# Order of the expert blocks in the mixture-of-experts stage: four pairs first, then one overflow block and one pair in turn

## What is computed

```python
g_val, g_idx = lax.top_k(g_prob, 1)                 # best of 4 groups
e_val, e_idx = lax.top_k(in_group, MOE_TOPK)        # two of its 4 experts
...
hid = jax.nn.silu(jnp.einsum('td,edf->tef', t, w1)) * jnp.einsum('td,edf->tef', t, w3)
out = jnp.einsum('tef,efd->td', hid * combine[..., None].astype(hid.dtype), w2)
```

## Time and profile before

| | |
|---|---|
| median of three runs | 1314.01 us |
| the profiled execution's own time | 1310.76 us |
| its span in the profile | 1308.9 us |
| mean granted TensorE clock | 0.97 |
| TensorE matmuls busy | 1189.5 us, 91% of the span |
| VectorE, ScalarE, GpSimd busy | 49%, 29%, 14% |
| DMA engines, share of the SP queue q1 | 49.9% |
| expert stage of layer 0, from up(0) to the end of down(12) | 603.8 to 758.8 us |
| the same of layer 1 | 1122.8 to 1279.1 us |

### The profile page before, as it was taken

The page is one execution under the profiler, slowest core; times in us unless marked ns, Lnnn a source line. Parts: engine busy times, 40 slices in busy tenths (PEclk is TensorE's granted clock), DMA queues, the critical chain, the costliest instruction groups (busy, mean ns, idle before and its releaser), DMA issues.

```text
span 1308.9 us, 15046 instructions
## 1 busy us (share of the span) xinstructions
PE 1189.5 (91%) x4903; PEld 638.3 (49%) x4903; DVE 645.2 (49%) x1372; ACT 376.2 (29%) x954; POOL 186.1 (14%) x281
## 2 busy tenths in 40 slices
PE   5999999999999999978999939999889897899990
PEld 3566665656666554444344424433554444344440
DVE  2367668667676643463233251068755425322223
ACT  2144444444443320021122122112264532121110
POOL 1012232323232330001000030011200000100002
PEclk9999999999999999998999969999989999999996
DMA  9941992643724625785999866000380015799976
GB/s 327 326 128 49 350 304 72 241 157 108 248 97 167 258 80 205 297 330 190 412 421 421 354 211 233 1 0 1 83 303 1 1 72 218 281 416 420 420 309 227
DMA packets 102714, 285.94 MB, mean 218 GB/s; under 512 B 18224, under 2 KB 51296, under 8 KB 86384
## 3 DMA queue, kind: packets, MB, share of 16 engines
q1 hardware_dynamic: 82816, 245.65, 49.9%
q10 hardware_dynamic: 13776, 22.57, 5.2%
q0 software_dynamic: 6048, 16.79, 3.6%
HBM read 270.24 MB, written 27.85 MB: 228 GB/s over the span
## 4 chain that ended last, share of the span: by engine, by line
PE 74%; DVE 8%; DMA 6%; ACT 3%; DVEq 3%; issue 2%; SPq 2%; POOL 1%; ACTq 1%; POOLq 0%
PE bank L738 60%; DMA wts<-in_moe_w 2%; PE bank L909 2%; PE bank L1200 2%; DVE work L1707 1%; DMA work<-in_ada_w 1%; ACT xn L1658 1%; PE bank L1087 1%; DMA work<-slot_rows,work 1%; DVE wts L1707 1%; PE bank L1251 1%; PE bank L1049 1%; DVE xn L2255 1%; SPq L453 1%; PE bank L1264 1%
## 5 line engine op out<-in xcount | busy, mean ns | idle before, releaser
L738 PE MATMUL bank<-wts 128*128 128x512 f32 (+1 forms) x1312 | 458.8, 501 | 0.5 <-DVE work L1707 0.5
L738 PE MATMUL bank<-wts,work 128*128 128x512 f32 (+1 forms) x1088 | 376.1, 595 | 14.8 <-DVEq L2096 6.8
L738 PEld LDWEIGHTS bank<-wts 128*128 128x128 f32 x1312 | 243.7, 190 | 178.5 <-issue 163.4
L738 PEld LDWEIGHTS bank<-wts,work 128*128 128x128 f32 (+1 forms) x1088 | 148.8, 166 | 216.1 <-issue 200.6
L1707 DVE SCALAR_TENSOR_TENSOR work<-work,bank 128x256 f32<-128x256 f32 x58 | 24.3, 419 | 183.8 <-ACT work L1552 162.8
L1334 ACT ACTIVATE work<-bank 128x512 f32<-128x512 f32 (+2 forms) x120 | 62.8, 538 | 167.0 <-PE bank L738 125.4
L738 PE MATMUL bank<-work 128*64 128x512 f32 (+2 forms) x336 | 104.8, 576 | 6.6 <-DVE work L2065 4.9
L1707 DVE SCALAR_TENSOR_TENSOR work<-work 128x512 f32<-128x512 f32 (+4 forms) x121 | 93.8, 776 | 27.9 <-ACT work L1621 20.5
L1707 DVE SCALAR_TENSOR_TENSOR wts<-wts,cond 128x1024 f32<-128x1024 f32 x68 | 87.8, 1292 | 4.1
L1552 ACT ACTIVATE work<-bank 128x256 f32<-128x256 f32 x26 | 10.0, 384 | 226.7 <-PE bank L738 226.7
L696 POOL DMA_INDIRECT work<-xn_rows,work x26 | 26.1, 1005 | 261.6 <-PE bank L1087 217.0
(11 more groups left out here) (233 smaller groups left out, 1291.5 us busy)
## 6 DMA issues: line engine op xcount, KB each, us to landing
wts<-in_moe_w SPq DMA_DIRECT2D x90, 1024.0 KB, 23.1
wts<-in_ada_w SPq DMA_DIRECT2D x10, 4096.0 KB, 13.3
work<-in_moe_w SPq DMA_DIRECT2D x24, 1024.0 KB, 24.5
wts<-in_ssd_w_in SPq DMA_DIRECT2D x15, 1024.0 KB, 11.3
slot_rows<-work ACTq DMA_DIRECT2D x26, 512.0 KB, 7.8
xn<-in_moe_w SPq DMA_DIRECT2D x12, 1024.0 KB, 16.1
wts<-in_ssd_w_in SPq DMA_DIRECT2D x16, 512.0 KB, 12.4
work<-running_sums ACTq DMA_DIRECT2D x32, 256.0 KB, 3.6
```

Source lines behind the costliest of these rows:

```text
L738: return pe.matmul(out, lhsT, rhs, start=(k == 0), stop=(k == n - 1))
```

## The change

The tuple `BLOCK_AT` alone is altered. Everything that is derived from it follows: the slots, the order of loads, of gathers and of products.

```diff
-BLOCK_AT = (0, 1, 2, NP, 3, NP + 1, 4, NP + 2, 5, NP + 3, 6, NP + 4, 7) + tuple(range(NP + SURE, NB))
+BLOCK_AT = (0, 1, 2, 3, NP, 4, NP + 1, 5, NP + 2, 6, NP + 3, 7, NP + 4) + tuple(range(NP + SURE, NB))
```

## The result

The changed kernel took 1317.09 us (median of 8, 1316.6 to 1318.39) against 1314.43 of the kernel before (8 runs, 1312.59 to 1315.96), a ratio of 1.0022 with a 95% interval of 1.0012 to 1.0032. A second set of runs gave 1.0035 (1.0022 to 1.0048). Of 1314 us these ratios are 2.9 and 4.6 us. So the change makes the kernel slower, by 3 to 5 us, where I had said 9.6. The direction and the place were right, the size was too large by a factor of 3.3 against the one and 2.1 against the other.

What follows compares the result with a forecast made beforehand. Late in both expert stages TensorE and the DMA engines were taken as full at once, so the loads' lead counts. Terms 3.0 + 3.5 + 3.1 = 9.6 us on 1310.76 give 1320.4, or 1323.5 as median; range 1317 to 1328.

Steps and rivals of the forecast that it cites:

- The mechanism: End of both expert stages: up(11) comes to need load 39 instead of 36 and waits, by 3.0 and 4.8 us; up(12) does not wait.
- "Place 12" in layer 0: Expert stage of layer 0: up(12) begins at 745.0 instead of 741.96, +3.0 us, passed to the end in full.
- I keep the landing times of before by number: Weight loads of both layers: each load number lands when it did before, since only its number in the queue sets its landing.
- no load is issued later than the one of its number before: Weight loads of both layers: the same slots or more are free at each place; no size given.
- rival (d): DMA queue: deeper reserve fills holes, so neither place 11 nor 12 waits; -1.4 us at most, 1312.6; chance 0.03.
- Rival (c): Place 11: load 39 lands as its row says, at 731.5 and 1251.7; together +2.5 us, 1316.5; chance 0.10.
- low reading of a w1's landing: Load 39 before, a w1: reads only 0.8 and 0.7 us behind load 38; early parts of load 40 may fill its count.
- Place 12 in layer 1: Expert stage of layer 1: up(12) begins at 1265.8 instead of 1262.32, +3.5 us, the old wait of 1.32 us gone.
- The clock term: TensorE behind the gap at up(11): clock drops in layer 1, +3.1 us; 0 in layer 0, with 3.1 kept for the range.
- The sum: Whole kernel: 3.0 + 3.5 + 3.1 = 9.6 us slower, 1323.5 us; chance of this forecast 0.40.

## Why the prediction was right and where it was wrong

**The mechanism** was as predicted: the end of the order moves the last load that place 11 needs from number 36 to 39, up(11) waits for it in both layers, and up(12) no longer waits. No other place waits for a load in either profile, place 9 included, for which I had allowed up to 0.5 us. The run with the end alone exchanged and the run with places 3 to 10 alone show that only the end costs anything. The runs with lighter loads show that nothing but the supply carries the cost, the low clock behind the wait included.

**The term "Place 12" in layer 0**, +3.0 us, is the largest error in proportion. The stage became 1.3 us longer. The landing of load 39 was set too late by 1.3 us (129.4 against 128.1 after up(0)), and up(11) was ready 0.3 later than in the earlier trace rows (730.76 - 603.97 = 126.8 against 730.28 - 603.79 = 126.5), so the gap was 1.4 and not 3.0. When a wait is the difference of two nearly equal times, an error of 1% in one of them halves it.

**The step that failed** first is the sentence that I keep the landing times of before by number, with what it rests on, that only the number of a load in the queue sets its landing. Number sets the landing closely, as the run with the end alone shows (both waits within 0.05 us). It did so there because the front part was that of before. With the new front part load 39 landed 1.3 us earlier than I had taken in layer 0 and 0.6 in layer 1, and load 40 1.6 and 0.6 us earlier than in the mean of the four profiles of before. The lead is there early: load 14 lands at 50.6 and 53.0 us, against 51.9 to 54.3 and 53.4 to 54.1 before. I had read from the earlier trace rows that the DMA engines are busy throughout, but these rows show the late part alone. Windows over the first 20 us from up(0) of layer 0, before and changed:

```profile
603.79:623.79 20.00, 18.34 (x92) 7.95 (x94) 5.25 (x18) 4.17 (x11) 1.98 (x3) 1.00 0.60 234
```

```profile
603.97:623.97 20.00, 18.34 (x92) 7.93 (x94) 5.26 (x18) 4.17 (x11) 1.99 (x3) 1.00 0.64 251
```

The engines are busy for 0.60 of this time, so here the queue is not long, and the new order fills part of the hole: 17 GB/s more over 20 us are 0.34 MB, which at 420 GB/s is 0.8 us (an estimate from these rows). All four profiles of before have 232 to 234 GB/s there, both of the changed kernel 251. In layer 1 it is 313 to 325 against 337 and 338. Two things move into the hole. The first load is issued 7.1 us after up(0) instead of 7.8, since no expert number has to be read for it, and load 2 lands 0.7 us earlier. And the gather for place 3 moves the rows of a pair, 476 KB in layer 0, where it moved 68 KB before. The first alone is not enough. With all pairs first, load 1 is issued at 7.1 as well, but load 14 lands at 53.8 and 55.2 us. There the gathers of places 3, 4 and 5 are all those of pairs, where the changed kernel has two of them. So the gathers on the way count too, and not the number of the load alone. How the gain divides between the two is not shown. Nor is it true that no load is issued later than the one of its number before: loads 5 and 13 are issued 0.7 us later. They landed no later for it.

This is what rival (d) had in mind, loads that come earlier because the DMA had holes. It had the direction right, and of the 3 and 4.8 us that it needed 1.3 and 0.6 came. The prediction had also priced loads that are 1 us faster, with 1 us less in layer 0 and little in layer 1, and for layer 0 that is roughly what happened.

**Rival (c)** is not what happened, although its total of +2.5 us lies near the timed difference. It needed the w3 at number 39 to land less than 0.9 us behind load 38, with gaps of 1.3 and 2.6 us. The waits were 1.41 and 3.80. The first is near its number, but for another reason, the earlier loads. From load 37, a w3 too, to load 39 it took 5.4 us in layer 0 and 4.9 in layer 1, so about 2.6 us for each load. And load 40, on which the reading was built, ended the wait of up(11) in the run with the end exchanged at the time that its row gives. So the low reading of a w1's landing, which the rule on shared semaphores of the Trainium skill ("DMA: Bandwidth & Descriptors", section "Why a DMA increments its semaphore by 16 and not by 1") would explain, was rightly not used. That the rule is the reason was not tested by itself.

**Place 12 in layer 1**, +3.5, was mis-sized too. The stage became 4.2 us longer, of which 1.7 are the low clock (8.78 - 7.09), so 2.5 are the later start. The earlier landing of load 39 is 0.6 of the missing 1.0.

**The clock term**, +3.1, is the second step that failed. A low clock did follow the gap of layer 1 and none that of layer 0, as forecast. But I had carried over the 7 us of the earlier trace rows, which stand behind thin work, as the upper bound and taken nearly all of it. Here the low clock held for about half of that, and cost 1.7 us. Filling the gap took 1.5 us off the stage.

**The sum.** Instead of 3.0 + 3.5 + 3.1 = 9.6 the profiles show 1.3 + 2.5 + 1.7 = 5.5 us. I had added the sum to the median of before, which was right to do: the profile it was read from, at 1310.76, is 1 to 5 us shorter than the other three (1312.0 to 1315.3), because of the clock between the stages and other stretches that the change does not touch. The timed ratios give 2.9 and 4.6 us. The second agrees with 5.5 within its interval, the first reaches only 4.2. Why those eight runs show 2.6 us less than the stages of two profiles stays open. In the other kernels the two agree better. The two stages together differ from those of before by 30.7 us with all pairs first, where the runs give 30.7 too, by 14.7 against 16.4 (13.9 to 18.9) with the end exchanged, by 4.1 against 3.9 with the gap filled, by -0.9 against -0.3 with places 3 to 10 alone, and by -2.0 against -2.1 and -0.3 against -1.2 in the old and the new order with lighter loads in layer 1.

**Price and noise.** I gave 0.83 to slower by over 0.2%. The first ratio is 0.22%, with an interval that reaches below it, the second 0.35%. That the range from 1317 holds the median of 1317.09 is luck. Its lower end stood a little above rival (c), and I had not thought of a mixture of a smaller wait and a shorter low clock, which is what happened.

## What to carry to other kernels

Where the loads are supplied as fast as the products use them up, count for each product the number of the load that it needs in the queue's own order. An order that asks for two experts at the next to last place instead of the last one moves that number forward without moving the work. Exchanging the last two blocks alone then cost 1.25% here, and the whole new order 0.2 to 0.35%. When a stall is the small difference of two large times, give its whole range, and take the landing times from a run with the new front part before believing a size. Read the DMA share from the start of the stage on, and not in its late part alone: in the first 20 us here it was 0.60, and there the time of issue and the gathers shifted the landings behind them.

## What was not expected of the hardware

The length of an idle gap does not alone decide whether the granted clock falls. Behind the gap of 3.80 us it fell for 3.4 us and not for 7 as in the earlier trace rows. Behind that of 7.55 us with the end exchanged it was low for 6.8 us, but half of these lay inside the gap, and up(11) took only 1.5 us more. In layer 1 of the run with all pairs first a down behind a gap of only 1.96 us was slow, 5.35 us for 16 matmuls instead of 3.65, while the 2.65 of the earlier trace rows and the 2.17 in layer 0 of the same run left it at 2.4 GHz:

```profile
1258.15 5.35 PE L738 MATMUL bank<-wts,work 128*64 128x512 f32 x16 [1.96 <-DMA wts<-in_moe_w]
```
